# Router products from transposes of the unnormalised rows, and a gather straight from the residual

## The reference

```python
    mix = jnp.concatenate([o_diff, o_nat], axis=-1) @ w_out[l]
    x = x + gt1 * rms_norm(mix, g_post_mix[l])
    h2 = rms_norm(x, g_pre_ffn[l]) * (1.0 + sc2) + sh2
    f = moe_ffn(h2, w_router[l], b_router[l], w1[l], b1[l], w2[l], b2[l])
    x = x + gt2 * rms_norm(f, g_post_ffn[l])
# in moe_ffn
    logits = (hf @ w_router + b_router).astype(jnp.float32)
    top_val, top_idx = lax.top_k(logits, TOP_K)          # 4 of 32 experts
    gates = jax.nn.softmax(top_val, axis=-1)
    # tokens sorted by expert, padded; every expert: 1024 -> 2048, clamped SwiGLU, -> 1024
    hh = xb @ w1[e] + b1[e]
    return swiglu_clamped(hh) @ w2[e] + b2[e]
```

## Time and profile before

| | |
|---|---|
| median of 3 runs | 1451.95 us (1451.94 to 1452.36) |
| profiled execution | 1452.42 us, span of its trace 1450.6 us |
| TensorE, VectorE, ScalarE busy | 1305.5, 532.9, 400.4 us |
| router chain, output product's last matmul to logits | about 517.0 to 528.5 us |
| expert passes | about 538 to 1440 us, 53 passes |
| last half piece landed | about 1438.3 us |

### The profile page before, as it was taken

One profiled execution on the slowest core, in us unless ns is written; L12 is line 12 of the kernel. 1 busy time (PEld: TensorE's weight loads), 2 busy tenths in 40 slices (PEclk: granted clock), 3 DMA queues, 4 the chain that ended last, 5 costly groups with the idle time before them and its releaser, 6 DMA issues.

```text
span 1450.6 us, 32869 instructions
## 1 busy us (share of the span) xinstructions
PE 1305.5 (90%) x13166; PEld 787.8 (54%) x13166; DVE 532.9 (37%) x1085; ACT 400.4 (28%) x745; POOL 0.2 (0%) x4
## 2 busy tenths in 40 slices
PE   9999999999999988999999899787997879978896
PEld 8998679998688653343444344232442324423343
DVE  6833677885597752212121121111211211111122
ACT  6734444553455641111111111010110111111112
POOL 0000000000000000000000000000000000000000
PEclk9999999999999999999999999999999999999999
DMA  9431975555772599999999999999999999999995
GB/s 365 175 117 59 402 318 202 188 194 198 265 321 110 216 392 429 427 426 428 428 426 427 428 426 428 427 427 427 427 428 426 428 428 427 426 430 427 427 427 243
DMA packets 36527, 508.47 MB, mean 351 GB/s; under 512 B 4080, under 2 KB 4208, under 8 KB 5488
## 3 DMA queue, kind: packets, MB, share of 16 engines
q1 hardware_dynamic: 36432, 507.08, 83.9%
HBM read 506.02 MB, written 1.05 MB: 350 GB/s over the span
## 4 chain that ended last, share of the span: by engine, by line
PE 60%; DMA 25%; DVE 7%; ACT 5%; issue 3%; SPq 0%; DVEq 0%; ACTq 0%
PE acc L1278 19%; DMA low<-in_w 16%; PE acc L510 9%; PE acc L1297 8%; DMA high_part<-in_w 7%; PE acc L1268 3%; PE acc L1235 3%; PE acc L973 2%; PE acc L548 2%; DMA low<-in_stream 2%; PE acc L1242 1%; PE acc L549 1%; DVE w_lo L1477 1%; ACT high_part L1894 1%; PE acc L893 1%
## 5 line engine op out<-in xcount | busy, mean ns | idle before, releaser
L1278 PE MATMUL acc<-low,high_part 128*32 128x512 f32 x2384 | 285.7, 607 | 48.1 <-DMA low<-in_w 34.0
L2480 DVE TENSOR_SCALAR high_part<-acc 128x256 f32<-128x256 f32 x53 | 22.5, 425 | 506.9 <-PE acc L1278 506.9
L1278 PEld LDWEIGHTS acc<-low,high_part 128*32 128x32 f32 x2384 | 85.7, 110 | 203.2 <-issue 144.2
L1297 PE MATMUL acc<-low,high_part 128*32 128x256 f32 x2624 | 152.1, 381 | 10.1 <-DMA low<-in_w 10.1
L1892 ACT ACTIVATE high_part<-high_part 128x256 f32<-128x256 f32 x53 | 22.1, 416 | 469.5 <-DVE high_part L2480 469.5
L1477 DVE TENSOR_TENSOR w_lo<-low,w_hi 128x4096 fp32r<-128x4096 f32 (+1 forms) x30 | 130.5, 4353 | 35.9 <-ACT w_hi L1471 35.6
L1278 PE MATMUL acc<-high_part 128*32 128x512 f32 x1008 | 121.5, 610 | 18.5 <-DMA high_part<-in_w 14.9
L1297 PEld LDWEIGHTS acc<-low,high_part 128*32 128x32 f32 x2624 | 80.7, 110 | 74.8 <-DMA low<-in_w 13.3
L1471 ACT ACTIVATE w_hi<-low 128x4096 fp32r<-128x4096 f32 (+1 forms) x28 | 99.8, 3569 | 54.7 <-DMA low<-in_stream 49.0
L1268 PE MATMUL acc<-high_part 32*128 32x256 f32 x864 | 77.1, 425 | 15.1 <-ACT high_part L1909 11.6
L510 PE MATMUL acc<-x_hi,w_hi 128*128 128x256 f32 x352 | 85.4, 284 | 0.8 <-DVE x_lo L1505 0.7
(11 more groups left out here) (494 smaller groups left out, 1800.2 us busy)
## 6 DMA issues: line engine op xcount, KB each, us to landing
low<-in_w SPq DMA_DIRECT2D x140, 2048.0 KB, 34.5
high_part<-in_w SPq DMA_DIRECT2D x51, 2048.0 KB, 34.4
low<-in_stream SPq DMA_DIRECT2D x41, 2048.0 KB, 8.0
high_part<-in_stream SPq DMA_DIRECT2D x4, 2048.0 KB, 12.0
high_part<-in_natb SPq DMA_DIRECT2D x1, 2048.0 KB, 13.3
low<-in_w SPq DMA_DIRECT2D x2, 1024.0 KB, 41.9
high_part<-in_rows SPq DMA_DIRECT2D x1, 1536.0 KB, 14.2
high_part<-in_x SPq DMA_DIRECT2D x2, 512.0 KB, 4.6
```

The source lines that it names most:

```text
L1278: last = mm(flat[32 * q:32 * q + 32, 2048:2560], XG[:, b, 32 * kk:32 * kk + 32], wp[:, 2048 * b + 512 * q:2048 * b + 512 * q + 512], start ...
L1297: last = mm(flat[32 * q:32 * q + 32, 2816:3072], AT[:, 128 * (c % 2) + 32 * (c // 2):128 * (c % 2) + 32 * (c // 2) + 32], wp[:, 1024 * (c ...
L2480: ts(GLU, flat[:, 2048:2304], 7.0, None, ALU.min).then_inc(S("glu"), 1)
```

## The change

It has six parts.

1. Picks of sc2 and sh2 (four small products) and their copy move from behind the output product into the attention part: TensorE right behind `turn(1)`, ScalarE behind `evac(1)`. `GW2`, `STACK` and three fills move on VectorE ahead of the output product's evacuation.
2. TensorE transposes the residual rows without the root (`turn_rows`, into the other two banks) as soon as each half is there; the evacuation has only the scale: VectorE takes three half tiles in one operation each, ScalarE one in four.
3. The shift goes through the router's weights: nine products (128x32) of a broadcast column add sh2 @ w_router and the bias, ScalarE copies the result over the bias. VectorE multiplies the logits with the root and adds that.
4. The transposes back into rows and `H2R` are gone. The gather reads `X`, and `SEL` has the root instead of 1.
5. Scale and shift come behind the gather, in every pass: where ScalarE copied the gathered columns, VectorE multiplies them with `GW2` and adds sh2 (`scaled_rows`), behind the SwiGLU and ahead of the bias row.
6. SP asks for piece 8 behind the router products and for piece 9 behind the logits.

The core of the diff:

```diff
+            for k in range(KC):
+                mm(flat[:, 2624:2656], MODC[:, 16 + k:17 + k].broadcast_to([P, P]), wr[:, k, :], start=(k == 0), stop=False)
+            mm(flat[:, 2624:2656], ident[:, 0:1].broadcast_to([P, P]), vec("brt"), start=False, stop=True).then_inc(*signal("shb"))
+            turn_rows(0)
             pe.wait_ge(S("by_gate"), 2)
-            picks(2, 5).then_inc(*signal("modc2"))
-            keep_busy(7, 3, NLASTING)
             gate_rows(1, 6)
-            pe_norm_by_tile()
+            turn_rows(1)
...
+            for t, b in ((0, 0), (1, 0), (1, 1)):
+                v.wait_ge(S("xT"), 4 * 3 + 2 * t + b + 1)
+                ks, o = slice(4 * b, 4 * b + 4), 1024 * (1 - t) + 512 * b
+                tt(HT[:, ks, 128 * t:128 * t + 128], three(flat[:, o:o + 512], 4), GW2[:, ks].unsqueeze(2).broadcast_to([P, 4, P]),
+                   ALU.mult).then_inc(S("hT_dve"), 1)
...
+            for t in range(T):
+                last = stt(LG[:, t, :], flat[:, 2560 + 32 * t:2592 + 32 * t], rstd[:, t:t + 1], vec("brt"), ALU.mult, ALU.add)
...
-                    last = ts(SEL[:, t, :], slot[:, 0:CAP], PP[:, t, bass.ds(p, 1)], None, ALU.is_equal)
+                    last = ts(SEL[:, t, :], slot[:, 0:CAP], PP[:, t, bass.ds(p, 1)], rstd[:, t:t + 1], ALU.is_equal, ALU.mult)
...
+            def scaled_rows(p):
+                def by_column(ap):
+                    return ap.rearrange("p (q b) -> p b q", b=2).unsqueeze(3).broadcast_to([P, 2, 4, CAP])
+                got, rows = flat[:, 3584:3840].rearrange("p (b q i) -> p b q i", b=2, q=4), XG.rearrange("p b (q i) -> p b q i", q=4)
+                v.wait_ge(S("h"), p + 1)
+                tt(rows, got, by_column(GW2), ALU.mult).then_inc(S("xg_scaled"), 1)
+                v.wait_ge(S("xg_scaled"), p + 1)
+                tt(rows, rows, by_column(MODC[:, 16:24]), ALU.add).then_inc(S("xg"), 1)
```

More of the change, by code:

```diff
@@ L455, in pe_norm, with turned, turn_rows @@
                     last.then_inc(S("xT"), 1)
[L457 to L465, removed]
+        def turned(t, k):
+            return flat[:, 1024 * (1 - t) + 128 * k:1024 * (1 - t) + 128 * k + 128]
+        def turn_rows(t):
+            for k in range(KC):
+                if k % 4 == 0:
+                    nc.tensor.wait_ge(S("x4"), 2 * t + k // 4 + 1)
+                last = nc.tensor.transpose(turned(t, k), X[:, t, 128 * k:128 * k + 128], ident)
+                if k % 4 == 3:
+                    last.then_inc(S("xT"), 1)
         def hT_ready(pe, i):
@@ L1129, in _ @@
             turn(1)
+            pe.wait_ge(S("modr"), 3)
+            picks(2, 2).then_inc(*signal("modc2"))
             score_pair(6)
@@ L1181, in _ @@
             out_lo(1, 1)
-            pe.wait_ge(S("modr"), 3)
+            wr = three(vec("router"), KC)
+            pe.wait_ge(S("by_gate"), 1)
+            for k in range(KC):
+                mm(flat[:, 2624:2656], MODC[:, 16 + k:17 + k].broadcast_to([P, P]), wr[:, k, :], start=(k == 0), stop=False)
+            mm(flat[:, 2624:2656], ident[:, 0:1].broadcast_to([P, P]), vec("brt"), start=False, stop=True).then_inc(*signal("shb"))
+            turn_rows(0)
             pe.wait_ge(S("by_gate"), 2)
-            picks(2, 5).then_inc(*signal("modc2"))
-            keep_busy(7, 3, NLASTING)
             gate_rows(1, 6)
-            pe_norm_by_tile()
-            wr = three(vec("router"), KC)
-            for b, evacuated in enumerate(("hT_dve", "hT_act")):
-                pe.wait_ge(S(evacuated), 2 * 1 + T)
+            turn_rows(1)
+            for b in range(2):
+                pe.wait_ge(S("hT_dve"), 2 * 1 + 2 + b)
+                pe.wait_ge(S("hT_act"), 2 * 1 + b)
                 for k in range(4 * b, 4 * b + 4):
@@ L1201, in _ @@
             last.then_inc(*signal("lg"))
[L1202 to L1207, removed]
+            keep_busy(0, 3, NLASTING)
             pe.wait_ge(S("gtb_in"), 2)
@@ L1234, in gather @@
                     for q in range(4):
[L1235 removed]
+                        last = mm(flat[32 * q:32 * q + 32, 3072:3328], SEL[:, t, :], X[:, t, 256 * q:256 * q + 256],
                                   start=(t == 0), stop=(t == T - 1))
@@ L1837, in square_out @@
                 a.wait_ge(S("out_done"), i + 1)
-                f((bank(1), bank(2), bank(3), XN[:, 1, 512:1024])[i], bank(OUT_BANKS[i]), ACT.Square,
+                f((bank(1), XN[:, 1, 0:512], bank(1), XN[:, 1, 512:1024])[i], bank(OUT_BANKS[i]), ACT.Square,
                   accum_out=ssq[:, i:i + 1]).then_inc(S("ssq"), 1)
@@ L1852, in _ @@
             root("m", 1)
+            a.wait_ge(S("xT"), 4 * 3 + 2)
+            for k in range(4, KC):
+                last = f(HT[:, k, 0:128], turned(0, k), ACT.Copy, scale=GW2[:, k:k + 1])
+            last.then_inc(S("hT_act"), 1)
+            a.wait_ge(*step("shb"))
+            f(vec("brt"), flat[:, 2624:2656], ACT.Copy)
             for i in range(4):
@@ L1856, in _ @@
             root(4, 1)
[L1857 to L1862, removed]
             a.wait_ge(*step("lgp"))
@@ L2396, in _ @@
             v.wait_ge(*step("lg"))
-            tt(LG, three(flat[:, 2560:2624], T), vec("brt").unsqueeze(1).broadcast_to([P, T, NE]), ALU.add).then_inc(S("logits"), 1)
+            v.wait_ge(S("rstd"), ROOTS.index((4, 1)) + 1)
+            for t in range(T):
+                last = stt(LG[:, t, :], flat[:, 2560 + 32 * t:2592 + 32 * t], rstd[:, t:t + 1], vec("brt"), ALU.mult, ALU.add)
+            last.then_inc(S("logits"), 1)
             v.wait_ge(S("logits"), 1)
@@ L2424, in _ @@
             for t in range(T):
-                last = ts(SEL[:, t, :], slot[:, 0:CAP], PM[:, t, 0:1], None, ALU.is_equal)
+                last = ts(SEL[:, t, :], slot[:, 0:CAP], PM[:, t, 0:1], rstd[:, t:t + 1], ALU.is_equal, ALU.mult)
             last.then_inc(S("sel"), 1)
```

50 lines of the change are left out of this document (17 added, 33 removed).

## The result

The changed kernel takes 1456.14 us (median of 10 runs, 1452.59 to 1458.04) against 1452.41 of the kernel before (10 runs, 1451.94 to 1453.95): ratio 1.0023, 95% interval 1.0014 to 1.0032. It is 3.3 us slower by the ratio; the forecast was 1450.8 with a range up to 1454.3. The profiled execution took 1456.84 us, span 1455.1.

The account below looks back on a forecast made before the run. The prediction took the unbroken expert-weight stream (427 GB/s, about 545 to 1436 us) as the bound. Terms -1.8 + 0.25 + 0.43 = -1.1 us took the median from 1451.95 to 1450.8; range 1449.2 to 1454.3.

Parts of the forecast that it names:

- Router chain, -1.8: Ahead of the experts: logits end 1.7 to 1.9 us sooner, the weight stream resumes earlier; -1.8 us, bounds -0.8 to -2.8.
- Moved picks and constants, 0: Attention part and front: moved picks, copy and small VectorE operations fall into existing waits; cost 0, outer bound +0.3 us.
- Handover from pass to pass, d = 0.55: Between passes of the same expert: VectorE's multiply and add delay TensorE by 0.55 us each time, bounds 0.15 to 1.1.
- The rival that was to be dearer here: Between passes: handover costs more than the router gives; 1453.6 us at 0.95 each, 1454.7 at 1.1; chance 0.20.
- Handover from up to down, "hidden by 0.2": Up-part followed by its predecessor's down-part: columns ready at 577.1, needed at 577.35, so no cost.
- The sum at 676.5, +0.25: Tightest weight-piece issue: five pass handovers, 2.75 us, against a slack of 2.4 to 2.5; +0.25 us.
- The issue of 734.2, put at nothing: Next tightest weight-piece issue: 12.7 us from issue to landing, enough for six pass handovers; no cost.
- no later issue has less than 21 us: Weight-piece issues after 734.2: each has at least 21 us from issue to landing, so none adds cost.
- The end, +0.43: Program end: two pass handovers behind TensorE's wait at 1358.51, partly absorbed by its last waits for pieces; +0.43 us.
- The waits of 0.23 and 0.44: Program end: TensorE's waits for pieces at 1433.54 and 1435.91; their disappearance was a sign the forecast was right.

Follow-up runs that it names:

- e1: Changed kernel with ScalarE copying the gathered columns as before and no scaled rows; their scale and shift left out: 1451.03 us, ratio 0.9988.
- e2: Changed kernel with VectorE reading the down-part's first pass and number of passes ahead of the up-part's loop: 1452.27 us, ratio 1.000.
- e3: Kernel before plus two spare 128x256 VectorE operations behind the bias row in each pass, on a tile nobody reads: 1455.39 us, ratio 1.0018.
- e4: Kernel before plus the two spare VectorE operations a pass, with the down-part's numbers read ahead of the up-part's loop: 1452.24 us, ratio 1.000.
- e5: Changed kernel plus two filler products on TensorE ahead of the third expert: 1455.11 us, ratio 1.0015.
- e11: Changed kernel plus two filler products ahead of the third expert, run again beside the changed kernel on one chip: 1455.11 us, ratio 1.0014.
- e8: Changed kernel with down-part numbers read early and one VectorE operation a pass; shift of the gathered columns left out: 1450.97 us, ratio 0.9989.
- e9: Changed kernel with gathered columns scaled in halves and bias row ahead of the SwiGLU; no filler, numbers not read early: 1454.94 us, ratio 1.0018.
- e7: Changed kernel with early down-part numbers, filler ahead of the third expert, columns in halves and bias row ahead of the SwiGLU: 1451.10 us, ratio 0.9988.

## Why the prediction was wrong

**Router chain, -1.8: mechanism right, size too small.** The program measured -2.5 at the logits and -2.4 at the twelfth piece. The sum let ScalarE carry the chain with copies of 0.36 and squares that end at 524.4; the four copies took 1.14/4 = 0.285, and the last accumulator was read at 523.86. The twelfth piece landed 1.5 us earlier (546.6 instead of 548.2). Near 561 the landings are 2.9 us ahead, but 1.45 of that is the one late landing at 559.4 in the profile of before, which is luck of that profile. Without the scaled rows the medians gain 1.7 us (e1).

**Moved picks and constants, 0: right** as far as the profile goes; the output product ends 0.2 us later (517.3 instead of 517.2), and what that is due to is open.

**Handover from pass to pass, d = 0.55: right to the hundredth.** The rival that was to be dearer here did not come: the far end of the range was passed by another way.

**Handover from up to down, "hidden by 0.2": this is the step that failed.** It compared the scaled columns with the transposes that need them (577.35) and stopped there. That holds: these transposes still start 0.64 behind the scatter. But behind the scaled rows on the same engine stand the loop's end, two reads (two steps of the sequencer each, 0.19 to 0.32 a step in the chain above), the next loop's head and the AT copy. The sum gave this part nothing. The profile books the reads as `issue` or as sequencer rows, not as work, and the cover over them was thin: the idle 1.62 us before the copy at 577.84 looks like a wait for the scatter, but the sequence needs all of it, and TensorE came only 0.24 to 0.43 behind the copy. Put 0.9 in front, and 0.45 to 0.75 is left as TensorE's wait, for each of 30 experts. e2 takes it away in the changed kernel (3.9 us by the medians), e3 and e4 put it into the kernel before and take it out again (+2.6 us by the ratio, then 0).

**The sum at 676.5, +0.25.** Forecast: 5 x 0.55 against a slack of 2.5. In the profile TensorE came to the third expert's pass 2.4 us early, lost 1.7 to the clock and 0.7 to the first late AT copy (at 578.38), and stood at 582.44, exactly as before; it then saved the 0.79 it used to wait at 588.80 and about 0.2 more. From there 5 x 0.55 + 2 x 0.65 = 4.05, less 1.0: 3.05 against 3.0 measured. The stream, 1.5 ahead at the landing before (680.2), fell 0.5 behind (687.1).

**The issue of 734.2, put at nothing.** Six handovers from pass to pass (3.3) and four late AT copies (2.5), less the 1.0, make 4.8 us; it measured 5.1 (739.3), against a slack of 12.7 - 7.7 = 5.0. So this issue was too late as well. The landing behind it is 2.2 behind before's (749.1 against 746.9), and it stays there. The prediction's reading that no later issue has less than 21 us is wrong in one place (736.0 has 15.8), which changes nothing.

**The end, +0.43.** TensorE's last wait for a piece is the first of three rows of its timeline, after; it answers to 1358.51 in the earlier trace rows:

```profile
1360.62 3.54 PE L1277 MATMUL acc<-high_part 128*32 128x512 f32 x16 [2.98 <-DMA high_part<-in_w]
...
1405.31 3.66 PE L1296 MATMUL acc<-low,high_part 128*32 128x256 f32 x64 [0.73 <-DVE high_part L2521]
...
1444.48 1.52 PE L1267 MATMUL acc<-high_part 32*128 32x256 f32 x16 [0.50 <-ACT high_part L1905]
```

It is 2.1 us late there and 4.5 late at the last scatter (1444.48, before 1439.97). Two handovers between passes make 1.1, three from up to down 0.66, 0.80 and 0.61, 0.17 lies between 1360 and the transposes of 1365, and 0.9 comes back where TensorE had waited for pieces: 2.4 instead of 0.43. The waits of 0.23 and 0.44 are gone, as predicted.

**The range** ended at 1454.3 because its dear end was a dearer d. The late reads alone, priced at 0.7 for each up-to-down handover, would have given: at 676.5 two more (1.4), at the end three more (2.1), so 1450.8 + 3.5 = 1454.3 without any fall of the clock. That is an estimate made after the runs. What is left of the measured 1456.1 is 1.8 us; about 1 of it went with the clock's fall in e5 and e11, as far as their medians can tell, and the rest is open.

## What to carry to other kernels

Work that is put at the end of a loop's body delays all that the engine does on leaving the loop, register reads included, and these show up as `issue` or in the sequencer's rows and never as a busy engine. Follow the program of the engine that gets the work up to the next instruction that another engine waits for, and look how much of the time in front of that was idle in earnest. Reads of trip counts belong ahead of a loop in which the engine waits anyway: here this alone was worth 3.9 us by the medians. And where a wait list puts a wait down to another engine, compare the idle time with places where that engine was surely not the last: here the 30 copies came 0.16 to 0.39 behind the semaphore and the others 0.15, and that was the sign, before the change, that the sequencer had no room left.

## What the runs showed of the hardware

VectorE's sequencer needed 1.43 to 1.64 us from the end of the bias row to the copy behind an exit from one loop, two reads of a register from SBUF and the entry into another, and 1.84 to 2.05 us where a semaphore wait stood in front of it (e3). With the reads out of the way the idle time was 0.40 to 0.50 in e2, and the scatter ended it. At the place of the chain above each read took two steps of 0.19 to 0.32.

In a chained pair of 128x256 operations the second started 0.46 us behind the first (591.57 and 592.03), and without it a pass was 0.47 shorter; one operation in ScalarE's place cost 0.08 (e8): it is the chain that is dear.

Ahead of the third expert TensorE's granted clock fell in five profiles, behind pauses of 1.36 to 1.51 us (the changed kernel twice, e2, e3, e4), and stayed up in four, behind pauses of 1.35 to 1.42 (before, e1, e8, e9). The length of the pause does not part them. The five are the kernels with two chained 128x256 operations of VectorE more in each pass, and the four are the ones without; whether that is the cause no run tells. The fall in the changed kernel cost 1.7 us of TensorE. In four profiles (e1, e3, e7, e11) it fell in the first pass instead or as well, and there the twelfth piece was asked for 0.9 to 1.7 us later than in the nearest kernel where it had not fallen.

In a stream that never runs dry the landings are 4.9 us apart, but six times in the profile of before one is 6.35 to 6.6 apart (559.4, 707.9, 875.7, 1043.6, 1221.4, 1394.3), 148 to 178 us from one to the next. The others have them too, some as two or more of 0.2 to 1.3 beyond the 4.9 instead of one of 1.5. The bytes do not pause with them: in the 6 us that end with each of the six the DMA engines moved 415 to 431 GB/s (by windows), where a stop of 1.5 us would leave about 320. So it is the last part of a piece that is late, and landings of two profiles can differ by 1.5 us without any difference in the stream. What makes it late is open.
